# A sparse attention layer's compression in a two-block kernel: keys and values stored residue by residue

## The reference

```python
def compress_blocks(a, idx, pos, w1, w2):
    blocks = a[:, idx] + pos[None, None, :, None, :]
    hdn = jax.nn.gelu(jnp.einsum('bclgd,ldf->bcgf', blocks, w1), approximate=True)
    return jnp.einsum('bcgf,fd->bcgd', hdn, w2)

n_cmp = (T - CMP_LEN) // CMP_STRIDE + 1                      # 31
cmp_idx = np.arange(n_cmp)[:, None] * CMP_STRIDE + np.arange(CMP_LEN)[None, :]
k_cmp = compress_blocks(kc, cmp_idx, pos_k, w1_k, w2_k)
v_cmp = compress_blocks(vc, cmp_idx, pos_v, w1_v, w2_v)
```

## Time and profile before

| | |
|---|---|
| median of 3 runs | 2934.8 us (2933.4 to 2935.02) |
| profiled execution | 2935.78 us, span 2934.0 us |
| TensorE busy | 2847.1 us, 97% |
| VectorE, ScalarE, GpSimd busy | 1442.1, 1060.2, 14.7 us |
| line 1358, TensorE | 128 records, 28.5 us busy |
| the stretch of `nsa_input` | about 774 to 925 us |

### The profile page before, as it was taken

The page is one execution under the profiler, slowest core; times in us unless marked ns, Lnnn a source line. Parts: engine busy times, 40 slices in busy tenths (PEclk is TensorE's granted clock), DMA queues, the critical chain, the costliest instruction groups (busy, mean ns, idle before and its releaser), DMA issues.

```text
span 2934.0 us, 38371 instructions
## 1 busy us (share of the span) xinstructions
PE 2847.1 (97%) x16336; PEld 2295.8 (78%) x16336; DVE 1442.1 (49%) x2335; ACT 1060.2 (36%) x1585; POOL 14.7 (1%) x29
## 2 busy tenths in 40 slices
PE   7987899999999999999999999999999999999998
PEld 5786678888787887888887888876788788888886
DVE  5733566553523664755436443364733444554432
ACT  5533444332323663433224222233433522332221
POOL 0000000000000000000000000001000000000000
PEclk9999899999999999999999999999999999999999
DMA  4200022222331001222222222236222122232221
GB/s 144 80 15 3 22 87 93 94 93 93 127 112 58 1 1 58 86 94 94 94 94 83 95 95 94 94 109 111 87 83 83 65 94 93 65 115 93 94 93 65
DMA packets 67965, 238.81 MB, mean 81 GB/s; under 512 B 7848, under 2 KB 8872, under 8 KB 67284
## 3 DMA queue, kind: packets, MB, share of 16 engines
q1 hardware_dynamic: 60912, 219.36, 22.3%
q10 hardware_dynamic: 6884, 17.00, 2.5%
HBM read 228.23 MB, written 6.03 MB: 80 GB/s over the span
## 4 chain that ended last, share of the span: by engine, by line
PE 92%; DVE 4%; ACT 3%; issue 1%; DMA 0%; ACTq 0%; DVEq 0%
PE psum L149 24%; PE psum L151 24%; PE psum L150 24%; PE psum L1068 3%; PE psum L172 2%; PE psum L1047 2%; PE psum L1055 2%; PE psum L173 2%; PE psum L181 2%; PE psum L667 2%; PE psum L1358 1%; PE psum L1567 1%; PE psum L1709 1%; PE psum L1745 1%; PE psum L673 1%
## 5 line engine op out<-in xcount | busy, mean ns | idle before, releaser
L149 PE MATMUL psum<-x_hi,w_hi 128*128 128x512 f32 x2184 | 884.5, 405 | 3.2 <-issue 1.6
L151 PE MATMUL psum<-x_hi,w_lo 128*128 128x512 f32 x2184 | 867.8, 397 | 0.0
L150 PE MATMUL psum<-x_lo,w_hi 128*128 128x512 f32 x2184 | 867.5, 397 | 0.0
L124 DVE TENSOR_TENSOR w_lo<-raw,w_hi 128x1024 fp32r<-128x1024 f32 x409 | 499.6, 1224 | 361.9 <-ACT w_hi L117 361.9
L117 ACT ACTIVATE w_hi<-raw 128x1024 fp32r<-128x1024 f32 x409 | 427.6, 1049 | 335.1 <-DMA raw<-w_down 84.4
L149 PEld LDWEIGHTS psum<-x_hi,w_hi 128*128 128x128 f32 x2184 | 412.8, 189 | 110.1 <-issue 9.8
L150 PEld LDWEIGHTS psum<-x_lo,w_hi 128*128 128x128 f32 x2184 | 413.1, 189 | 102.5 <-issue 5.3
L151 PEld LDWEIGHTS psum<-x_hi,w_lo 128*128 128x128 f32 x2184 | 412.8, 189 | 100.6
L149 PE MATMUL psum<-h_hi,w_hi 128*128 128x512 f32 x704 | 280.7, 399 | 0.0
L151 PE MATMUL psum<-h_hi,w_lo 128*128 128x512 f32 x704 | 279.1, 396 | 0.0
L150 PE MATMUL psum<-h_lo,w_hi 128*128 128x512 f32 x704 | 279.1, 396 | 0.0
(11 more groups left out here) (376 smaller groups left out, 2999.6 us busy)
## 6 DMA issues: line engine op xcount, KB each, us to landing
raw<-w_up SPq DMA_DIRECT2D x88, 512.0 KB, 3.3
raw<-w_down SPq DMA_DIRECT2D x44, 512.0 KB, 3.3
raw<-w_f1up SPq DMA_DIRECT2D x44, 512.0 KB, 3.3
raw<-w_f2up SPq DMA_DIRECT2D x44, 512.0 KB, 3.3
raw<-w_qkv SPq DMA_DIRECT2D x36, 512.0 KB, 3.3
raw<-w_blend SPq DMA_DIRECT2D x28, 512.0 KB, 3.3
raw<-w_f1down SPq DMA_DIRECT2D x22, 512.0 KB, 3.3
raw<-w_f2down SPq DMA_DIRECT2D x22, 512.0 KB, 3.3
```

What stands on the lines that cost most here:

```text
L124: dve.tensor_tensor(self.w_lo[u % SLOTS][:], self.raw[u % SLOTS][:], self.w_hi[u % SLOTS][:].bitcast(F32), ALU.subtract).then_inc(self.lo_ ...
L149: pe.matmul(bank[:], hi, x_hi[:, kk], start=kk == 0, stop=False)
L150: pe.matmul(bank[:], hi, x_lo[:, kk], start=False, stop=False)
L151: mm = pe.matmul(bank[:], lo, x_hi[:, kk], start=False, stop=kk == kt - 1)
```

## The change

`z`'s tiles of compression keys and values are written by VectorE in another order of tokens: token 16n + b goes to column 32b + n, so residue b's 32 tokens lie side by side. The reads of PSUM and of `rn` go on in token order; the writes are 32 elements (128 bytes) apart. The other 17 tiles are written as before.

The copies to `wide` take this order along. "16 tokens later" is one column further now, so the upper half is a copy of 1,023 columns starting at column 1 of each pair of tiles. At the end of each residue the column of the neighbouring residue or group falls in; it belongs to block 31. Only the very last column of a pair has nothing to be copied: GpSimd clears it for the first pair, and in the second pair the position terms go there.

The position terms have a buffer of their own, `pos[s]`, and GpSimd copies their 16 columns into the last column of the last group, once for each residue, after all four copies have landed (`moved[s]`) and the loads too. TensorE waits for that copy (`posed`) where it waited for `moved[s]`. The moving operand of a matmul is now four runs of 32 neighbouring columns, one run for each group; 128 columns instead of 129, of which the last is the bias.

```diff
-SEGS = NG * T // 16 + 1
+SEGS, SEG = NG * T // 16, T // 16
@@ act
-                    act.dma_start(mem.wide[s][HD:P, c].rearrange("p (a n) -> p a n", a=2)[:, :, 0:T - 16],
-                                  src[:, :, 16:T]).then_inc(moved[s], 16)
+                    act.dma_start(mem.wide[s][HD:P, c.start:c.stop - 1],
+                                  src.rearrange("p a n -> p (a n)")[:, 1:2 * T]).then_inc(moved[s], 16)
...
-                    act.activation(mem.hid[:, s, ft], seg[:, ft, 0:SEGS - 1], ACT.Gelu_apprx_tanh,
+                    act.activation(mem.hid[:, s, ft], seg[:, ft], ACT.Gelu_apprx_tanh,
@@ pe
-                pe.wait_ge(moved[s], 64)
-                view = mem.wide[s][:].rearrange("p (n b) -> p b n", b=16)
+                pe.wait_ge(posed, s + 1)
+                view = mem.wide[s][:].rearrange("p (c b n) -> p b c n", c=NG, b=16)
@@ dve
-            dve.scalar_tensor_tensor(out=z[:, NSA_ORDER[i]], in0=k.bank(g, i)[:], scalar=k.v("scale1", NSA_ORDER[i]), in1=k.rn[:],
+            f = NSA_ORDER[i]
+            out, product, factor = z[:, f], k.bank(g, i)[:], k.rn[:]
+            if ZKC <= f < ZKC + 4:
+                out = out.rearrange("p (b n) -> p n b", b=16)
+                product, factor = (x.rearrange("p (n b) -> p n b", b=16) for x in (product, factor))
+            dve.scalar_tensor_tensor(out=out, in0=product, scalar=k.v("scale1", f), in1=factor,
                                      op0=ALU.mult, op1=ALU.mult).then_inc(k.bank_free, 1)
@@ pool
-            pool.memset(mem.wide[s][HD:P, 0:NG * T].rearrange("p (a n) -> p a n", a=NG)[:, :, T - 16:T], 0.0).then_inc(cleared, 1)
+            pool.memset(mem.wide[s][HD:P, 2 * T - 1:2 * T], 0.0).then_inc(cleared, 1)
...
+        pool.wait_ge(loaded_k, 16 * 5)
+        for s in range(2):
+            pool.wait_ge(moved[s], 64)
+            last = mem.wide[s][:].rearrange("p (c b n) -> p c b n", c=NG, b=16)[:, NG - 1, :, SEG - 1]
+            pool.tensor_copy(last, mem.pos[s][:]).then_inc(posed, 1)
@@ load
-            sp.dma_start(mem.wide[s][:, NG * T:NG * T + 16], dram[f"in_pos_{n}"]).then_inc(loaded_k, 16)
+            sp.dma_start(mem.pos[s][:], dram[f"in_pos_{n}"]).then_inc(loaded_k, 16)
@@ buffers
-                N.wide = [sb(f"nsa_wide{j}", [P, SEGS * 16], stack=s2) for j in range(2)]
-                N.hid, N.hb = sb("nsa_hid", [P, 2, 2, SEGS - 1], stack=s2), sb("nsa_hb", [P, 2, 2], stack=s2)
+                N.wide = [sb(f"nsa_wide{j}", [P, NG * T], stack=s2) for j in range(2)]
+                N.pos = [sb(f"nsa_pos{j}", [P, 16], stack=s2) for j in range(2)]
+                N.hid, N.hb = sb("nsa_hid", [P, 2, 2, SEGS], stack=s2), sb("nsa_hb", [P, 2, 2], stack=s2)
```

More of the change, by code:

```diff
@@ L1296, in nsa_input @@
         sem(f"nsa_{n}") for n in ("hidden", "opened", "made", "kept", "gates_turned", "gates_open", "valid", "cleared"))
+    posed = sem("nsa_posed")
     moved = [sem(f"nsa_moved{j}") for j in range(2)]
```

## The result

| | median, us | range | runs |
|---|---|---|---|
| before | 2934.8 | 2933.4 to 2935.02 | 5 |
| after | 2919.25 | 2916.04 to 2921.89 | 5 |

The ratio is 0.9945 with a 95% interval of 0.9932 to 0.9958, so the change gains 15.5 us, by the interval 12 to 20. The forecast was 2920.9 us, a gain of 13.9, in a range of 2919.0 to 2925.0. The median of the five runs lies just inside that range, and the ratio puts the time at 2918.7, outside it: the direction and most of the size were right, the range was not. Two executions of filled versions further down (b1 and b2) took 10787 and 5055 us at a granted clock of 0.55 and 0.76 and are counted nowhere.

A forecast was written before the change was run, and what follows sets the result against it. The prediction took the stage as bound by TensorE alone: compressions 28.14 to 14.2 us, a gain of 13.9, other terms hidden, so 2920.9 us from the median 2934.8; range 2919.0 to 2925.0.

The forecast's parts named there:

- The columns: Both compressions on TensorE: 128 records at 0.111 us, 14.2 us instead of 28.14, a gain of 13.9 us.
- VectorE's write: Strided write of four z tiles: about nothing more than 749 ns each; upper end 0.73 us more each, 2.9 in all.
- The cover: Slower z writes stay hidden: z of two tiles ends at 801.2, not 799.7; weights slide at most 1.5 us.
- Position terms and copies: Before the keys' compression: 0.2 us for GpSimd's copy and signal; upper copies land in 5.4 us as before.
- 2.2 us of cover: Position terms ready at 812.0, 2.2 us before TensorE comes to the keys' compression at 814.27.
- Behind 925 the whole rest is moved forward as it is: After the input product of the sparse layer, everything later just comes sooner, keeping the 13.9 us gain.
- the 1.6 us over which the runs scatter: Run-to-run scatter, used with the floor of 0.108 for the forecast's own range, 2919.5 to 2922.5 us.
- the floor of 0.108: Least us per compression record on TensorE, from 65 columns costing as much as 129: 13.8 us, a gain of 14.3.
- 1: Joints of the runs cost TensorE something: 0.138 us a record, gain 10.5, time 2924.3 us; chance 0.08.
- 2: The step isn't the cause; compression records stay at 0.218 us: gain 0.2, time 2934.6 us; chance 0.03.
- factor f: Slowdown of the upper copy's landing: TensorE waits 5.4 x (f - 1) - 2.2 us; gain gone at 4.0.
- rival 3: Odd start slows the upper copy, TensorE waits at 814.3: up to 2945.7 us; chance 0.02 in full, 0.02 partial.

The follow-up runs named there:

- b1: Changed kernel with idle matmuls filling TensorE's three pauses (start and end of the attention, first recurrence gate): 2913.96 us, ratio 0.9923.
- b2: Kernel before the change with idle matmuls filling TensorE's same three pauses: 2930.97 us, ratio 0.9982.
- a4: Changed kernel with VectorE writing all 21 tiles of z in token order again, the rest unaltered: 2920.26 us, ratio 0.995.
- a1: Changed kernel measured again without an edit: 2918.7 us, ratio 0.9948.
- d3: Changed kernel measured once more without an edit: 2920.03 us, ratio 0.9951.
- b4: Changed kernel with the compressions' four halves reading wide at steps 1, 2, 4, 8: 0.1116, 0.1134, 0.2266, 0.233 us a record.
- c3: Changed kernel with the compressions' four halves reading wide at steps 3, 4, 16, 2: 0.172, 0.227, 0.218, 0.1134 us a record.
- c2: Changed kernel with VectorE reading PSUM and rn every 16th element and writing neighbours in the four tiles: 2921.45 us, one run.
- a2: Changed kernel with both compressions computed twice: 2939.2 us, 0.15% slower than the kernel before.
- b3: Changed kernel with both compressions computed twice and TensorE's three pauses filled with idle matmuls: 2927.76 us, ratio 0.9974.
- c1: Changed kernel with upper copies starting 64 bytes into z, in one run of 1,008 columns: 2922.15 us, one run.

## Why the prediction was right and where it was wrong

*The columns*: right, 13.86 us against 13.9. The spacing in the chain, from another line with as many columns, was the right price, not the mean of one.

*VectorE's write*: taken at nothing, cost 0.36 to 0.44 us a tile, between the two bounds. The row I trusted, the reduction at line 1179, was no equal: another instruction with another length. The cover held, as a4 shows.

*Position terms and copies*: 0.2 us taken for GpSimd's copy, and 5.4 for the landing, as before the change. In a1 and d3 they are 0.21 and 5.7 us, and of the 2.2 us of cover 1.9 and 2.1 are left: the terms were right. In the first profile they are 0.65 and 7.4, and the cover shrank to 0.8 us and still held.

*Behind 925 the whole rest is moved forward as it is*: this step failed. In the first pair of profiles the rest gave 3.3 us more: two half-clock stretches were 3.4 us long instead of 6.8, and a third fell more on a pause. In a1, with stretches of 6.8 us as before the change, it gave 0.3 us, from the first z write to the end. The prediction read the clock by slices of the whole span and had no term for such stretches. Why the changed kernel got the short ones in two profiles of three isn't shown.

With it failed the range: it took "the 1.6 us over which the runs scatter" from three runs. The lower end, 2919.0, is the gain of 14.3 at the floor of 0.108, 2920.5 us, less 1.5 for the scatter. The kernel before goes over 59 runs from 2929.7 to 2941.4 with a standard deviation of 2.5 us, and the changed one over 15 runs from 2916.0 to 2925.3. An estimate from it: the median of five such runs scatters by 1.25 x 2.5 / 2.24 = 1.4 us, so an end two of these below 2920.5, at 2917.7, would have been right. That the first measurement came out so low was in part luck: all 15 runs of the changed kernel have a mean of 2919.6 us, inside the range.

*What stays open.* The kernel before has a mean of 2934.8 us (59 runs beside a, b and d, standard error 0.3), the changed one of 2919.6 (15, 0.7): 15.2 us. With pauses filled, 2929.3 (19, 0.4) and 2914.1 (10, 0.7): 15.2 as well. The rounds ran on different chips, but the mean of the kernel before differs by only 0.6 us between them. The columns explain 13.9. Behind the first z write the filled pairs leave nothing beyond that, so their other 1.3 us, less than two of its standard errors, could only come from ahead of it, where nothing was changed and the arrival scatters by 8.8 us. In the unfilled pair the stretches add 0.3 or 3.3 us as they fall; what they add in the mean of many runs isn't measured, and neither is what sets their length.

*The rivals*: 1 and 2 are refuted by b4 and c3, 3 by c2. The factor f of rival 3 came out at 5.7 / 5.4 in a1 and d3 and at 7.4 / 5.4 in the first profile, and by its own sum either is covered. The chances were sound; the range wasn't.

**A better version.** The changed kernel with its pauses filled takes 2914.0 and 2914.2 us, 5.5 us less than the changed kernel by the means and 20.7 less than the one before. It was made to test the clock and is the fastest found.

## What to carry to other kernels

Here an fp32 operand of 128 columns that TensorE read 16 bytes or more apart cost twice the time of neighbours; look for such a step by the spacing of the records in the chain, against a line with as many columns, and let an engine with time to spare do the scattering. Don't take a kernel's scatter from three runs: behind TensorE's pauses of 1.4 to 3.4 us the half-clock stretch differed from run to run. To compare two versions by their profiles, subtract the time at the last point up to which they do the same work: here that turned 17.0 and 14.1 us into 13.9 and 13.7. Filling such pauses with idle matmuls was worth 5.5 us here.

## What the runs showed of the hardware

*GpSimd waits for VectorE.* The copy of 128x16 takes 0.21 us in most profiles, but 0.65 and 1.12 in the changed kernel's first, 0.78 in a2 and 0.54 in b3. Each of these begins inside a w_lo subtraction of VectorE and ends 0.06 to 0.08 us behind it; in the timeline above 814.16 against 814.08, and 820.54 against 820.48. The Trainium skill ("SBUF — State Buffer", section "SBUF: two separate sides") has the two share a pair of ports, which a VectorE operation with two inputs in SBUF holds for its whole length against a GpSimd operation that reads there. These rows agree: of the other 24 copies in the profiles none begins within such a subtraction, but for one in b4 that begins 0.05 us before its end, and all take 0.21 or 0.22 us. In c1 no w_lo runs beside it:

```profile
809.52 0.21 POOL L1426 COPY nsa_wide<-nsa_pos 128x16 f32<-128x16 f32 x1 [12.23 <-DMA nsa_wide<-z]
...
816.29 0.21 POOL L1426 COPY nsa_wide<-nsa_pos 128x16 f32<-128x16 f32 x1 [6.56 <-DMA nsa_wide<-z]
```

*VectorE pays for a step too, but less.* 512 elements read at 64-byte steps, from PSUM and SBUF both (c2), or written to SBUF at 128-byte steps (the change) take 1.06 to 1.19 us instead of 0.70 to 0.75, where TensorE doubles.

*The same pause, another stretch.* Behind the pause of 2.25 us at the attention the half clock lasted 3.4, 6.8, 10.2 or 13.7 us in the profiles of this case, and no filled version had one there.
